# Two-layer hybrid decoder trunk: where the split weights lie in SBUF, 32 instead of 64 bytes past a multiple of 128

## The reference

```python
# layer 0: recurrent block, then dense SwiGLU (1024 -> 3584 -> 1024)
h = h + rglru_mixer(rmsnorm(h, norm_mix[0]), ...)
h = h + (silu(hn @ ffn_w_gate) * (hn @ ffn_w_up)) @ ffn_w_down
# layer 1: sliding-window attention with sinks, then top-2-of-8 experts
h = h + swa_sink_mixer(rmsnorm(h, norm_mix[1]), ...)
for e in range(8):
    out = out + comb[..., e:e+1] * ((silu(hn @ w_gate[e]) * (hn @ w_up[e])) @ w_down[e])
h = h + out
return rmsnorm(h, norm_final)
```

## Time and profile before

| | |
|---|---|
| median of 3 runs | 1501.08 us (1499.4 to 1502.77) |
| the profiled execution | 1497.96 us |
| its span, first to last instruction | 1496.0 us |
| TensorE busy (matmul / weight load) | 1458.1 us (97%) / 1333.8 us (89%) |
| VectorE, ScalarE, GpSimd busy | 1161.5, 916.6, 42.7 us |
| moved by DMA | 426.14 MB, mean 285 GB/s |
| granted TensorE clock, mean | 0.990 of full speed |

### The profile page before, as it was taken

How to read it: one execution, slowest core, us unless ns; L and a number is a source line. 1 busy time by engine, 2 the same in 40 slices (tenths; PEclk the granted TensorE clock), 3 DMA queues, 4 the chain that set the end, 5 groups by cost and what they waited for, 6 DMA issues and landing times.

```text
span 1496.0 us, 25391 instructions
## 1 busy us (share of the span) xinstructions
PE 1458.1 (97%) x10682; PEld 1333.8 (89%) x10682; DVE 1161.5 (78%) x1094; ACT 916.6 (61%) x904; POOL 42.7 (3%) x62
## 2 busy tenths in 40 slices
PE   8999999999899999999999999999999999999996
PEld 7889999998888989899888989989989898998885
DVE  6676555557545998887889788888889888878896
ACT  3744443443434776676767676667676766767675
POOL 2020000003001000000000000000000000000000
PEclk9999999999998999999999999999999999999999
DMA  8465555544207999999899999999989989999940
GB/s 325 144 224 196 190 193 176 195 170 142 85 29 310 389 385 345 358 351 341 340 362 374 335 347 353 341 341 356 373 301 377 357 328 354 351 340 338 364 185 30
DMA packets 60000, 426.14 MB, mean 285 GB/s; under 512 B 7024, under 2 KB 7152, under 8 KB 8688
## 3 DMA queue, kind: packets, MB, share of 16 engines
q1 hardware_dynamic: 58752, 422.60, 75.7%
q10 hardware_dynamic: 1136, 1.91, 0.4%
HBM read 423.44 MB, written 1.05 MB: 284 GB/s over the span
## 4 chain that ended last, share of the span: by engine, by line
PE 91%; DVE 4%; ACT 2%; issue 1%; POOL 1%; DMA 0%; DVEq 0%; ACTq 0%; SPq 0%; POOLq 0%
PE ps L1807 39%; PE ps L1829 21%; PE ps L1507 11%; PE ps L1529 5%; PE ps L1429 2%; PE ps L1795 2%; PE ps L1569 2%; PE ps L1777 2%; PE ps L1672 1%; PE ps L1814 1%; DVE w_lo L823 1%; DVE w_lo L1237 1%; ACT w_hi L656 1%; PE ps L1616 1%; PE ps L1444 1%
## 5 line engine op out<-in xcount | busy, mean ns | idle before, releaser
L1237 DVE TENSOR_TENSOR w_lo<-ring,w_hi 128x2048 fp32r<-128x2048 f32 x336 | 765.9, 2289 | 122.7 <-ACT w_hi L656 117.5
L656 ACT CAST w_hi<-ring 128x2048 fp32r<-128x2048 f32 x336 | 639.7, 1909 | 263.3 <-PE ps L1807 211.5
L1807 PE MATMUL ps<-w_hi,xg_hi 128*96 128x256 f32 x1792 | 247.2, 280 | 1.2 <-DVE xg_lo L1243 1.2
L1807 PE MATMUL ps<-w_lo,xg_hi 128*96 128x256 f32 x1792 | 243.2, 278 | 1.1 <-DVE w_lo L1237 0.7
L1807 PE MATMUL ps<-w_hi,xg_lo 128*96 128x256 f32 x1792 | 242.6, 277 | 0.0
L1807 PEld LDWEIGHTS ps<-w_hi,xg_hi 128*96 128x96 f32 x1792 | 222.4, 161 | 15.1 <-DVE xg_lo L1243 1.3
L1807 PEld LDWEIGHTS ps<-w_lo,xg_hi 128*96 128x96 f32 x1792 | 216.1, 161 | 2.7 <-DVE w_lo L1237 2.7
L1807 PEld LDWEIGHTS ps<-w_hi,xg_lo 128*96 128x96 f32 x1792 | 216.6, 161 | 0.0
L823 DVE TENSOR_TENSOR w_lo<-ring,w_hi 128x2048 fp32r<-128x2048 f32 x56 | 129.8, 2319 | 80.7 <-ACT w_hi L471 80.6
L471 ACT CAST w_hi<-ring 128x2048 fp32r<-128x2048 f32 x56 | 106.5, 1903 | 111.7 <-PE ps L1507 92.5
L1829 PE MATMUL ps<-w_hi,ht_hi 128*96 128x512 f32 x448 | 128.1, 408 | 0.0
(11 more groups left out here) (275 smaller groups left out, 1333.9 us busy)
## 6 DMA issues: line engine op xcount, KB each, us to landing
ring<-in_moe_w_gate SPq DMA_DIRECT2D x112, 1024.0 KB, 5.8
ring<-in_moe_w_up SPq DMA_DIRECT2D x112, 1024.0 KB, 5.8
ring<-in_moe_w_down SPq DMA_DIRECT2D x112, 1024.0 KB, 5.8
ring<-in_ffn_w_gate SPq DMA_DIRECT2D x14, 1024.0 KB, 4.7
ring<-in_ffn_w_up SPq DMA_DIRECT2D x14, 1024.0 KB, 4.9
ring<-in_ffn_w_down SPq DMA_DIRECT2D x14, 1024.0 KB, 4.8
ring<-in_lru_w_in SPq DMA_DIRECT2D x7, 1024.0 KB, 12.5
ring<-in_attn_w_qkv SPq DMA_DIRECT2D x6, 1024.0 KB, 4.8
```

The costliest lines, as they stand in the source:

```text
L656: nc.scalar.copy(w_hi[:, (SPLITS + n) % PARTS], ring[:, s]).then_inc(hi_done, 1)
L1237: V.tensor_tensor(w_lo[:, part], ring[:, ORDER_MOE[n % SLOTS]], w_hi[:, part].bitcast(F32), ALU.subtract).then_inc(lo_done, 1)
L1807: mm = nc.tensor.matmul(ps[0:CAP, c % 2, m * CHF:(m + 1) * CHF], xs[a][:, k], w[b][:, k], start=(k == 0 and (a, b) == (0, 0)), stop=(k == ...
```

## The change

The two unused tiles around the split weights change size: the one ahead of them from 16 to 8 columns, the one behind them from 16 to 24.

```diff
         ring = sb("ring", [P, SLOTS, SLOT])
-        gap = sb("gap", [P, 16])
+        gap = sb("gap", [P, 8])
         w_hi, w_lo = sb("w_hi", [P, PARTS, SLOT], F32R), sb("w_lo", [P, PARTS, SLOT], F32R)
-        gap2 = sb("gap2", [P, 16])
+        gap2 = sb("gap2", [P, 24])
         h = sb("h", [P, KC, T])
```

## The result

The changed kernel takes 1511.17 us (median of 5 runs, 1508.61 to 1512.89), the kernel before 1499.75 us beside it (5 runs, 1498.94 to 1502.77). The ratio is 1.0074, 95% interval 1.0063 to 1.0085: 11 us slower, slight but clear.

The account below looks back on a forecast made before the run. The prediction took PE's matmul pace as the bound. Writers 0 and PE's reads 0 added to the profiled 1497.96 us, put on the median's scale, gave 1501.1 us; the range was 1490 to 1526, for 8 in 10.

Parts of the forecast that it names:

- the case that I held likeliest: Whole kernel: the placement does nothing, 1501 us, no change within 0.2%; chance 0.47.
- What bounds the kernel: PE, busy 97% of the span: time is the number of matmuls times the pace of one.
- Writers of the split weights at 0: ACT casts into w_hi and DVE subtractions into w_lo cost 0 more, staying at 1.91 and 2.29 us.
- The argument from `xpad`, `z_lo` and `asq`: ACT and DVE instructions at other offsets show the same times, so reads and writes at 32 were costed at 0.
- PE's reads at 0: Matmuls that stream or hold w keep their pace at offset 32: 0 us, bounded by +23 to 28 and -17.
- The first rival: Matmuls streaming w: rows off a multiple of 64 bytes take one unit more, about 1526 us; chance 0.16.
- The second rival: Shifting w against xg and u changes which pace level holds: more short groups, 1484, chance 0.21; all long, 1510, 0.16.
- The way down: More groups at the short pace: expert stage gains 9 us (1492), with the dense stage 17 us (1484); chance 0.21.
- dense 11.31 towards 10.9: Sign of more short groups: 96 dense matmuls go from 11.31 us towards 10.9.
- the sign that I had set for the forecast itself: Prediction is wrong if any matmul streaming or holding w changes pace by more than 0.4 ns on average.

Follow-up runs that it names:

- e7: Kernel before with only u_hi, u_lo, f_hi and f_lo, the dense stage's streamed activations, moved by 64 bytes; ratio 1.0059.
- e9: Kernel before with the expert stage's held tiles xg and ht moved by 112 bytes; 1492.25 us against 1500.05, ratio 0.9931.
- e6: Kernel before with only ht_hi and ht_lo, the down product's held tokens, moved by 64 bytes; 1492.99 us against 1498.18, ratio 0.9966.

## Why the prediction was right, and where it was not

The median of 1511.17 lies in the range of 1490 to 1526, but not by the case that I held likeliest, no change and 1498 to 1504. The range holds it because it was drawn wide enough for the rivals.

- **What bounds the kernel**: right. PE's pace set the time, and the paces of the matmul groups follow the placements through fourteen kernels, with a remainder of some us in e7, which lies where the clock differed, and in e9, where it was not located.
- **Writers of the split weights at 0**: right. 2290 and 1909 ns, to a nanosecond. The argument from `xpad`, `z_lo` and `asq` held, for the write at 32 too, of which it had no row.
- **PE's reads at 0, "since the two offsets that are seen do not differ"**: this is the step that failed. I compared a stream of `u` at 0 with a stream of `w` at 64. But in every one of these matmuls the other operand was the one at the other offset: `w` held and `u` streaming, or `xg` held and `w` streaming, 64 apart each time. The rows held a single value of the variable that counts, and I read them as two. The right reading was that the trace has no contrast at all in it, and that the bounds should carry the weight. That 32 and 64 are both multiples of 16 bytes settled nothing either: every offset tried here is one.
- **The first rival (a 64-byte unit, 1526)**: wrong. Its sign that the dense 11.31 stays failed (11.36), the down groups it would have lengthened did not, and with the weights at 0 the kernel is slower still.
- **The second rival, the way up ("all groups long, gives + 9, 1510")**: this is what happened, with nearly its price. It took half of the groups to be short (48 of 110) and 0.16 us each; the long level came out at 5.60 to 5.61 instead of 5.62, and the stage lost 7.7 us. I gave it 0.16. Its ground, a shift of `w` against `xg` and `u`, was the mechanism; its argument against, that levels change without a change of address, was true and beside the point, since an offset can choose the pair of levels and leave the choice within the pair to what went before. The way down exists as well: e9 and e6 gained 10 and 5 us, and their expert stages 4.9 and 5.7 in the trace, of the 9 that were bounded for that stage.
- **The signs**: "dense 11.31 towards 10.9" did not come; the dense stage went the other way, by 0.05 us for 96. By the sign that I had set for the forecast itself, a pace changed by more than 0.4 ns on average, it is wrong: gate-and-up moved by 0.070 / 48 = 1.5 ns a matmul, the dense stage by 0.05 / 96 = 0.5 ns.

The Trainium skill (TensorE: Matmul & The Clock Gate, Wait — 56ns, not 53.3ns?) has back-to-back matmuls at columns over 2.4 GHz plus about 2.5 ns, which makes an estimate of 109.2 ns for 256. No group here reaches that; in the expert and the dense stage the paces run from 5.45 / 48 = 113.5 to 11.52 / 96 = 120 ns, and move with placement.

## What to carry to other kernels

When matmuls follow each other without a gap, look at where the held and the streamed tile begin modulo 128 bytes: here placement is worth almost 2% (ratios 0.9931 to 1.0125) with the same instructions, and moving the small tile works as well as moving the large one. Before arguing that a placement does not matter, ask which variable the rows at hand really vary; two operands at two offsets can be one and the same offset between them. After any change of placement count the groups at each pace, because part of the gain or loss comes from neighbours that were not touched.

## What the runs showed of the hardware

- At a granted clock of 1.00, 48 matmuls of 256 float32r columns with 96 held columns take 5.44 to 5.47 us at the shorter of their levels with held and streamed tile 64 or 80 bytes apart, 5.60 and 5.61 at 32 or 48, 5.60 and 5.68 at 0, 5.65 and 5.66 at 96. With 128 held columns and the other roles, 96 take 11.52 us at 0, 11.36 at 32, 11.31 at 64, and 11.27 or 11.39 at 96.
- The pace has levels that persist over whole groups and depend on what ran ahead: moving only the down product's tokens changed the gate-and-up groups from 48 to 77 short ones. At one placement they repeat from expert to expert.
- ScalarE's casts and VectorE's subtractions between these tiles took the same time at every placement, 1.91 and 2.29 us.
